# Latents, attention and the samples' queries of a hybrid decoder step in one block

## The reference

```python
q = rms_norm(concatenate([q[..., :D_NOPE], rope(q[..., D_NOPE:], positions)]), g_q)
ckv, kpe = rms_norm(ckv_raw, g_ckv), rope(kpe_raw, positions)
# prompt, per head
k = rms_norm(concatenate([ckv @ w_uk, kpe]), g_k)
sc = where(key_pos <= q_pos, (q @ k.T) * scale, -inf)
o = (softmax(sc) @ ckv) @ w_uv
# samples: the same over 2048 cached latents and the new one of each sequence
```

## Time and profile before

| | us |
|---|---|
| median of 3 runs (3179.08 to 3184.54) | 3179.48 |
| profiled execution / its span | 3183.28 / 3181.3 |
| PE busy / DVE / ACT / POOL | 2609.9 / 2124.5 / 907.7 / 1388.3 |
| gated norm's first load to latents' first load | 698.9 to 742.9 |
| latents, w_uk, first loads of the heads | 742.9 to 789.6 |
| eight heads | 789.6 to 1082 |
| samples' queries | 1082 to 1120.9 |
| merge, residual, experts | 1120.9 to 3181.3 |

### The profile page before, as it was taken

One profiled execution on the slowest core, in us unless ns is written; L12 is line 12 of the kernel. 1 busy time (PEld: TensorE's weight loads), 2 busy tenths in 40 slices (PEclk: granted clock), 3 DMA queues, 4 the chain that ended last, 5 costly groups with the idle time before them and its releaser, 6 DMA issues.

```text
span 3181.3 us, 37483 instructions
## 1 busy us (share of the span) xinstructions
PE 2609.9 (82%) x12048; PEld 1778.0 (56%) x12048; DVE 2124.5 (67%) x4057; ACT 907.7 (29%) x3581; POOL 1388.3 (44%) x1159
## 2 busy tenths in 40 slices
PE   3898996763788889969699999999999999947632
PEld 1898985752444555534366556666565555625620
DVE  3564876753455200126989898989898979985767
ACT  2331002131232210012244444445354544420110
POOL 1212221100000000004777877888777877784565
PEclk7998998886777699989899999999999999966566
DMA  3424664323001067347999999999999999999778
GB/s 140 110 72 140 202 196 132 98 83 103 12 24 35 0 186 232 96 147 264 389 390 356 358 370 369 370 361 357 381 353 387 337 394 341 386 345 398 266 278 310
DMA packets 378321, 776.88 MB, mean 244 GB/s; under 512 B 46417, under 2 KB 185682, under 8 KB 378089
## 3 DMA queue, kind: packets, MB, share of 16 engines
q0 software_dynamic: 154144, 562.17, 47.2%
q1 hardware_dynamic: 203002, 187.70, 18.5%
q10 hardware_dynamic: 20980, 24.63, 2.3%
HBM read 745.09 MB, written 29.50 MB: 243 GB/s over the span
## 4 chain that ended last, share of the span: by engine, by line
issue 23%; POOL 9%; DMA 9%; DVE 8%; PE 6%; ACT 1%; SPq 0%; POOLq 0%; DVEq 0%; ACTq 0%
DMA mix_u<-in_peer_u,mix_ids 7%; POOL mix_v L1807 5%; POOL mix_u L1798 4%; DVE mix_acc L2185 3%; DVE mix_u L2280 3%; PE mix_pair L1974 2%; PE mix_pair L1833 1%; DMA smp_w_out<-in_peer_keys 1%; PE mix_pair L1865 1%; PE mix_pair L1888 1%; PE mix_pair L1952 0%; DMA pag_kpe<-in_cache_kpe 0%; ACT L2083 0%; PE mix_pair L1840 0%; DMA mod_mul<-keep_ada 0%
## 5 line engine op out<-in xcount | busy, mean ns | idle before, releaser
L1865 PE MATMUL mix_pair<-pag_wx,pag_ckvT 128*128 128x384 f32 (+3 forms) x3072 | 967.2, 462 | 15.9 <-ACT mix_raw L2047 9.6
L2280 DVE CUSTOM_DVE_ANT_0 mix_u<-mix_u,mix_h 128x1024 f32<-128x1024 f32 x512 | 622.8, 1216 | 225.4 <-DMA mix_u<-in_peer_u,mix_ids 222.5
L1807 POOL DMA_INDIRECT mix_v<-in_peer_v,mix_ids x512 | 664.7, 1298 | 223.3 <-issue 160.8
L1865 PEld LDWEIGHTS mix_pair<-pag_wx,pag_ckvT 128*128 128x128 f32 x3072 | 566.3, 192 | 305.3 <-issue 33.7
L1798 POOL DMA_INDIRECT mix_u<-in_peer_u,mix_ids x512 | 587.3, 1147 | 257.0 <-issue 146.6
L2185 DVE SCALAR_TENSOR_TENSOR mix_acc<-mix_v,mix_coef,mix_acc 128x1024 f32<-128x1024 f32 x449 | 574.5, 1279 | 0.0
L2045 ACT ACTIVATE mix_pair<-mix_pair 128x128 f32<-128x128 f32 x1024 | 266.8, 261 | 204.7 <-PE mix_pair L1865 204.2
L1880 PE MATMUL mix_pair<-mix_v,mix_diag 128*128 128x512 f32 x236 | 128.0, 670 | 103.0 <-ACT mix_diag L2062 102.4
L2340 POOL MEMSET sqr_mask<- 8x64 f32 x1 | 0.1, 141 | 438.1 <-POOLq L509 438.1
L2054 ACT ACTIVATE mix_coef<-mix_dots 128x4 f32<-128x4 f32 x128 | 26.3, 205 | 577.0 <-DVE mix_dots L2280 576.9
L2045 ACT ACTIVATION_READ_ACCUMULATOR mix_pair<-mix_pair 128x1 f32 x1024 | 189.9, 185 | 0.0
(11 more groups left out here) (469 smaller groups left out, 4584.2 us busy)
## 6 DMA issues: line engine op xcount, KB each, us to landing
pag_ckv<-in_cache_ckv SPq DMA_DIRECT2D x128, 256.0 KB, 15.3
stp_w<-in_w_in SPq DMA_DIRECT2D x32, 512.0 KB, 4.8
mrg_w_ada<-in_w_ada SPq DMA_DIRECT2D x8, 2048.0 KB, 9.0
cnv_w<-in_w_in SPq DMA_DIRECT2D x26, 512.0 KB
keep_proj<-stp_out ACTq DMA_DIRECT2D x32, 260.0 KB, 2.9
ada_w_ada<-in_w_ada SPq DMA_DIRECT2D x4, 2048.0 KB, 11.2
stp_st<-in_state_ssm POOLq DMA_DIRECT2D x8, 1024.0 KB, 7.1
out_ssm_s<-stp_st POOLq DMA_DIRECT2D x8, 1024.0 KB, 7.1
```

Source lines behind the costliest of these rows:

```text
L1807: pool.indirect_dma_start(v[:, y % VR, :], None, v_rows, bass.IndirectOffsetOnAxis(at, 0)).then_inc(v_in[y % VR], 16)
L1865: last = pe.matmul(to, ckvT[:, g % 2, k, :], wx[:, k, lo:hi], start=(k == 0), stop=(k == KL - 1))
L2280: dve.tensor_tensor_reduce(u[:, r, :], u[:, r, :], h2[:, t % 2, :], 1.0, 0.0, ALU.mult, ALU.add, dots[:, t % 2, slot:slot + 1]).then_inc(u ...
```

## The change

`latents`, `fetch`, `prompt_attention` and `sample_queries` become one block, `attention`. Its inputs are loaded by `AttentionInputs`: the latents' part from `gated_norm`'s SP list ahead of the eighth z, the queries' part behind the last z. z has seven buffers, which lie in the space of the later keys. Keys and values are made by token tile t for all heads at once (8 + 8 products of 512 columns), so that a key's norm is a sum along the free axis (ACT squares, DVE reduces, [128, 8] root and reciprocal); the keys are scaled there and turned to channels. The gains of q and k are folded into one (`gg`). The queries are not normalised: sums of their squares come from products with 32-column matrices (`select`), and the inverse root goes, times the scale, into the exponential's scale operand (`rqs`) and the shift (`nrqs`). The swap of the rope is done by the loads. `load_latents` issues ten of them (raw 1 MB, w_uk 2 MB, kpe, its two swapped halves, sine and cosine twice each at 0.13 MB, the gain), `load_queries` seventeen (q_n 2 MB, q_r and q_sw together 2 MB in six, w_uv 2 MB, the samples' parts in three of 32-byte pieces, six gains). Heads are pipelined: scores of h + 1 stand around the turns of h.

```diff
-def latents(nc, A, K, M, proj, outs):
-def prompt_attention(nc, A, K, M, proj, oT):
-def sample_queries(nc, A, K, M, L, W):
-def fetch(nc, tag, W, tiles):
+QO = (3, 0, 1, 2)
+class AttentionInputs:
+    def load_latents(self, sp, A, proj):
...
+    def load_queries(self, sp, A, proj):
...
+def attention(nc, A, K, L, I, oT, spare, outs):
+            def keys(t):
+                n = rows(t)
+                if t:
+                    pe.wait_ge(k_scaled, t)
+                for c in range(2):
+                    for k in range(KL):
+                        last = pe.matmul(bank[c][0:n, :], ckvT[:, k, t * P:t * P + n], I.w_uk[:, k, c * 512:(c + 1) * 512], start=(k == 0), stop=(k == KL - 1))
+                last.then_inc(keyed, 1)
+            def query_sums():
...
+                for j in range(3):
+                    for i in range(H // 2):
+                        x = q_sq[:, 2 * i + j, 0:TP] if j < 2 else q_r_sq[:, i, :]
+                        last = pe.matmul(bank[6][WIDE * i:WIDE * i + WIDE, :], select[:, j, :], x, start=(j == 0), stop=(j == 2), skip_group_check=True)
+            def score(h, q):
+                if h:
+                    pe.wait_ge(exped, TT * (h - 1) + AT[q] + 1)
+                w, at = (q + 1) * P, h % 2 * ROPE
+                pe.matmul(bank[q][:, 0:w], I.q_n[:, h, q * P:w], k_n[:, h, 0:w], start=True, stop=False)
+                pe.matmul(bank[q][:, 0:w], I.q_r[at:at + ROPE, h // 2, q * P:w], k_r[at:at + ROPE, h // 2, 0:w], start=False, stop=True).then_inc(scored, 1)
+            def turn_probs(h):
+                pe.wait_ge(shared, TT * (h + 1))
...
+            def weigh(h):
...
+                for n, (at, k) in enumerate(((0, 0), (512, 1), (896, 3), (1024, 2))):
+                    pe.wait_ge(p_copied, 3 * h + (1, 2, 2, 3)[n])
+                    last = pe.matmul(bank[7][:, k * P:TP], v[:, k, h * DV:(h + 1) * DV], probsT[:, at:at + TP - k * P], start=(k == 0), stop=(n == 3), skip_group_check=True)
...
+            keys(0)
+            sample_sums()
+            query_sums()
+            pe.wait_ge(I.w_uv_in, 16)
+            values(0)
+            sample_latents()
+            turn_sums()
+            pe.wait_ge(s_rooted, 1)
+            turn_latents(0)
+            turn_samples()
+            pe.wait_ge(s_kept, 2)
+            pe.wait_ge(q_rooted, 1)
+            turn_keys(0)
+            for t in range(1, TT):
+                keys(t)
+                values(t)
+                turn_latents(t)
+                turn_keys(t)
+            keys(TT)
+            turn_latents(TT)
...
+            score(0, 3)
+            score(0, 0)
+            score(0, 1)
+            pe.wait_ge(newed, 1)
+            score(0, 2)
+            for h in range(H):
+                if h + 1 < H:
+                    score(h + 1, 3)
+                    score(h + 1, 0)
+                turn_probs(h)
+                if h + 1 < H:
+                    score(h + 1, 1)
+                    score(h + 1, 2)
...
+                weigh(h)
...
+                act.activation(probs[:, h % 2, PACK[q]:PACK[q] + w], bank[q][:, 0:w], ACT.Exp, bias=shift[:, q:q + 1], scale=rqs[:, q * H + h:q * H + h + 1],
+                               accum_out=total[:, q:q + 1]).then_inc(exped, 1)
...
+            def mean(t):
...
+                then(dve.tensor_reduce(ss[0:n, :], key_sq[0:n, :, :], X, ALU.add))
+                dve.tensor_scalar(ss[0:n, :], ss[0:n, :], kss[0:n, t:t + 1], None, ALU.add).then_inc(k_meaned, 1)
+            then(dve.tensor_tensor(I.q_sw, I.q_sw, table(I.sin), ALU.mult))
+            then(dve.tensor_tensor(I.q_r[:, :, :], I.q_r[:, :, :], table(I.cos), ALU.mult))
+            then(dve.tensor_tensor(I.q_r[:, :, :], I.q_r[:, :, :], I.q_sw, ALU.add))
-def gated_norm(nc, A, K, S, proj):
+def gated_norm(nc, A, K, S, proj, I):
...
-        NB = 3
+        NB, NS = 7, 3
                 if k >= NB:
                     sp.wait_ge(gated, k - NB + 1)
+                if k == NB:
+                    I.load_latents(sp, A, proj)
                 sp.dma_start(z[:, k % NB, :], proj[C_Z + k]).then_inc(z_in[k % NB], 16)
+            I.load_queries(sp, A, proj)
```

More of the change, by code:

```diff
@@ L441, in _ @@
[L441 to L448, removed]
@@ L451, in _ @@
         @block.scalar
         def _(act):
[L453 to L462, removed]
-            for s in range(2):
[L464 to L476, removed]
-                for k in range(KL):
-                    pe.transpose(psT[0:n, b, k * P:(k + 1) * P], M["ckvT"][:, k, t * P:t * P + n], K["ident"][:, :])
-                pe.transpose(psK[0:n, b, 0:ROPE], M["kpeT"][:, t * P:t * P + n], K["ident"][0:ROPE, 0:ROPE]).then_inc(moved, 1)
@@ new lines, in copy_weights, with squares @@
+            def copy_weights(h):
+                act.wait_ge(w_turned, h + 1)
+                act.activation(w_ukT[:, h, :], bank[4 + h % 2][:, :], ACT.Copy).then_inc(w_copied, 1)
+            def squares(t):
+                n = rows(t)
+                act.wait_ge(keyed, t + 1)
+                if t:
+                    act.wait_ge(k_meaned, t)
+                for c in range(2):
+                    last = act.activation(key_sq[0:n, 4 * c:4 * c + 4, :].rearrange("p h d -> p (h d)"), bank[c][0:n, :], ACT.Square)
+                last.then_inc(key_squared, 1)
@@ new lines, in _ @@
+            copy_latents(0)
+            for t in range(1, TT):
+                squares(t)
+                root(t)
+                copy_values(t)
+                copy_latents(t)
+            squares(TT)
+            root(TT)
+            copy_latents(TT)
+            for q in QO:
+                exponential(0, q)
+            for h in range(H):
+                if h + 1 < H:
+                    exponential(h + 1, 3)
+                    exponential(h + 1, 0)
+                copy_probs(h)
+                if h + 1 < H:
+                    exponential(h + 1, 1)
+                    exponential(h + 1, 2)
+                keep(h)
@@ new lines, in scale @@
+            def scale(t):
+                dve.wait_ge(k_rooted, t + 1)
+                then(dve.reciprocal(rk[:, :], root_k[:, :]))
+                if t >= 2:
+                    dve.wait_ge(k_turned, t - 1)
+                for c in range(2):
+                    then(dve.tensor_tensor(k_tok[:, t % 2, 4 * c:4 * c + 4, :], bank[c][:, :].rearrange("p (h d) -> p h d", h=4), wide(rk[:, 4 * c:4 * c + 4], NOPE), ALU.mult))
+                then(dve.tensor_tensor(kpe_k[:, t % 2], kpe_tok[:, t, :].unsqueeze(1).to_broadcast([P, H, ROPE]), wide(rk[:, :], ROPE), ALU.mult))
+                dve.sem_inc(k_scaled, 1)
@@ new lines, in _ @@
+            dve.scalar_tensor_tensor(qs[:, :, 0:TS], I.q_n[:, :, TP:T], gg_n[:, :], rs[:, :, :], ALU.mult, ALU.mult).then_inc(s_ready, 1)
+            scale(0)
+            for j in range(2):
+                dve.wait_ge(s_wide, j + 1)
+                dve.tensor_copy(q_wide[:, j, :], bank[4 + j][:, :]).then_inc(s_copied, 1)
+            dve.wait_ge(q_rooted, 1)
+            then(dve.reciprocal(rqs[:, :], root_q[:, :]))
+            then(dve.tensor_scalar(nrqs[:, :], rqs[:, :], -SCALE, None, ALU.mult))
@@ new lines, in _ @@
+            for t in range(1, TT):
+                mean(t)
+                scale(t)
+                copy_keys(t)
+            mean(TT)
+            dve.wait_ge(k_rooted, NTL)
+            then(dve.reciprocal(rk[0:TS, :], root_k[0:TS, :]))
+            dve.wait_ge(new_scored, 1)
+            dve.wait_ge(made, 5)
+            then(dve.tensor_tensor(L["new"][:, :, :], bank[2][0:TS, 0:TS * H].rearrange("p (b h) -> p b h", h=H),
+                                   rk[0:TS, :].unsqueeze(1).to_broadcast([TS, TS, H]), ALU.mult))
```

694 lines of the change are left out of this document (344 added, 350 removed).

## The result

The changed kernel took 2977.8 us (median of 4 runs, 2975.0 to 2981.0) beside 3180.6 for the kernel before on the same chip: ratio 0.936, 95% interval 0.934 to 0.938. 2987 was forecast. Its profiled execution took 2975.7 us, span 2973.8.

The account below looks back on a forecast made before the run. Hand-overs between engines and PE's clock were taken to bound the kernel. Stage terms put the merge's first load at 928 us instead of 1121, 193 less; from the 3179.5 us median that gave 2987, range 2968 to 3046.

Parts of the forecast that it names:

- Gated norm: Norm stage: ends at 747.7 us in place of 742.65, +5, bounds -4 to +12.
- the term of the ten loads: In the norm: the latents' loads, about 3.95 MB queued ahead of the eighth z, take 12.5 us; eighth z at 720.
- the late-loads rival: Norm's end: slow query loads keep SP issuing from 748 to 759 us, +11, 2998 us; chance 7%.
- keys(0): First token tile: eight key products, 6.9 us, taken as 8.5 because PE has just been idle.
- Packed sums: First tile: sums of the queries' squares by twelve 32-column products, 2.9 us; eight such products take 1.92.
- Tiles: Token tiles 1 to 3: 16 products and 16 turns on PE, 15.7 us each, 47 together.
- Heads: Pipelined heads: PE sets the pace at 9.3 us a head; seven periods, 65 us, after head 0.
- Clock: Allowance of +3 us for PE's clock at keys(0), keys(1) and head 0, where it has small gaps.
- the lower clock: Rival in the heads: PE's clock falls at head 0 and stays, 17.4 us a head, 3044 us; chance 17%.
- The hand-overs: Rival in the heads: the 7.7 us chain between engines is really 12, 19 us more, 3006 us; chance 12%.
- The table switch in the norm: Table load ahead of the first exponential: 1.28 us, no drain; with the skill's 1.38 us drain, 1.3 us later.
- The experts: Rival in the unedited experts' stage: longer gather waits give the gain back, 3191 us at 0.40 more per gather; chance 2%.

Follow-up runs that it names:

- the latents behind: The changed kernel with the latents' ten loads moved behind the last z in SyncE's queue; 226.1 us from the norm's first load to the merge's.
- the pause run: The changed kernel with one more unused 128x512 reciprocal on VectorE in each head, ahead of the shares; 30.6 us more in the heads.
- the filled kernel before: The kernel before with unused products in PE's two long waits of each head; 3143.3 us for 3185.1, ratio 0.986.
- the serial run: The changed kernel with its heads one after the other, no scores of the next head around the turns; heads 119.1 us for 77.2.

## Why the prediction was right

The mechanism held: the end was set by hand-overs and PE's clock, and with both gone PE's own work is the length of the heads. By its steps, places counted from the norm's first load, so that the 2.6 us ahead of it drop out:

- **Gated norm**, +5 forecast, +6.8 measured. The eighth z is used 23.1 us behind the first load (719.37 less 696.24) for 21.2 forecast, and from there to the end of the stage it is 27.4 for 27.7. So what was short is the term of the ten loads, which hold the eighth z back. SP's issues were named as a bound (and as the late-loads rival, +11) and not put into the sum. They ended 0.3 us ahead of DVE, so leaving them out cost some 0.1 us at most; that was luck, for nothing in the sum made it so. Either end can be the last: in four of the eight profiles with this norm's code the next block begins 0.31 us behind DVE's last scaling, in the other four DVE stands 0.45 to 1.34 us, until SP is done. With the latents behind, the wait alone is gone and nothing is won, as SP then ends at 53.3; with both gone the stage is 11.5 us shorter. SP's stall alone was not taken away, so what that would give isn't shown.
- **Latents**: 14.9 forecast, 14.3 measured (746.81 to 761.11). **keys(0)**: 8.5 and 8.8, for 7.03 at the upper level; the granted clock was 0.81 there. **Packed sums**: the 1.92 us for eight hold to the hundredth. **Tiles**: 15.7 and 15.5 (786.15, 801.64, 817.12, 832.70). Row of samples to head 0's scores: 9.5 and 8.3. Head 0's scores, behind the first load: 145.7 and 144.7. That this place came out within 0.9 us is in part luck: the norm is 1.7 late and the stages behind it are 2.6 early.
- **Heads**: 9.3 forecast, 9.08 measured, PE full; the changes of rows are 0.19 each. The exponential with a scale from a tile is 0.78 us for 512 columns (0.82 taken; 0.69 with a constant), off the path. The last round, from the turns of head 6 to those of head 7, has no scores of a next head in it, 7.6 us for 9.1: my seven equal periods were one too many by 1.5.
- **Clock**, +3 forecast beside keys(0): nothing. PE runs at 1.00 from 770 us, behind keys(0), through the last weighing.
- **The sum**: 229.2 forecast (698.85 to 928), 221.9 measured, 7.2 off: clock 3.0, periods 1.5, last round 1.5, first scores 0.9, the rest in the tail. With 2.6 ahead of the norm and 4.8 behind the merge it makes the 14.7 between the 2990.4 forecast for the profiled execution and 2975.7.

Of the rivals, the lower clock did not come, but the pause run shows how near it was: one wait of 1.84 us in a head was followed by it each time, though by three to ten microseconds of it and not by the whole head that the rival has. The Trainium skill (TensorE: Matmul & The Clock Gate, A second HAM failure mode: psum-queue depth-cycling) tells of frequent small idles between groups of matmuls that make the clock swing; the changed kernel cycles through eight banks without idling and doesn't swing (1.00 throughout), and the pause run, with waits of 1.84 to 4.6 us, does (0.50 and 1.00 in turn). The hand-overs need at most 7.57 us, the forecast's chain was 7.7. The table switch in the norm is a load of 1.28 us and the next activation 0.01 behind it (730.10, 731.39), as in the earlier trace rows; the drain that the Trainium skill adds (ScalarE: Activation LUTs, What ACT_TABLE_LOAD costs) doesn't show here either. The experts didn't give anything back: their DVE waited 218.7 us for gathers, for 222.5.

What made up the 200: from the latents to the merge PE's idle time fell by 85 us and its busy time by 121, and the norm took 6.8 more. Of the 121, some 45 are the clock in the heads (the estimate from the filled kernel before). The rest of the 121 (fewer and wider products, 603 recorded halves for 984, and the clock outside the heads) was not parted. In the kernel before, filling the waits was worth 42.6 us; in the changed one, taking the overlap away costs 41.9. Which edit gave how much of the idle time (the reciprocals over 128x512 and 128x520, the sample block, the loads between blocks) was not taken apart one by one; what is said of that is argued from the trace.

## What to carry to other kernels

A wait of TensorE can have two prices, its length and the clock behind it; ask of a wait whether other work can be put into it, even work that was made serial for tidiness, and price the stretch after it at both levels. When loads are prefetched from another stage's queue, look at when the queue's engine issues its last one: a block ends there too, and the order of small and large loads decides it. When a stage runs full on one engine, the small fixed costs inside it (here 0.19 us for each change between 128 and 64 rows) are next.

## What the runs showed of the hardware

- In the pause run, behind four waits of PE of 1.84 us, the granted clock was 0.50 for about ten microseconds of full work twice and for about three and a half twice. In the serial run, behind eight waits of 3.55 us, it was 0.50 for about three and a half six times and for about seven twice. The length of the wait does not tell how long the lower level lasts.
- SP's issue of one load of the attention mostly takes 0.4 to 0.8 us. With several MB queued ahead of it single issues take 2.6 to 4.7 us, a load in 32-byte pieces, one of 0.5 MB and one of a gain alike; others in the same stretch still take 0.6.
- The same unedited stages from the merge on took 2053 to 2064 us in the first two profiles and the last four runs, and 2104 to 2158 in the eight between, which ran on other chips than the last four. Whether the chip is the reason isn't shown; stages, not whole times, had to decide there.
